# A per-partition scale in the one-hot gate activation, and the first two gate tiles made after the plain phase, in a PEER/attention kernel

## The chip, the cores and the metric

The kernel runs on one core of one Trainium2 chip. The metric is the device time of one execution in microseconds; the time before is 941.41 us, the median of three runs (940.76 to 946.43).

## The reference, cut to what matters

One layer of a diffusion backbone: modulated RMSNorm, an input projection, three mixers, an output projection, and then the PEER feed-forward that this case is about. For 256 tokens `h`:

```python
q = (hb @ w_q).reshape(T, 8, 2, 128)
s = einsum('thpd,hpkd->thpk', q, sub_keys)      # two lists of 128 scores for each head
top_s, top_i = top_k(s, 16)
best_s, best_pos = top_k(cand_s, 16)            # of the 16 x 16 sums
expert = cand_i[best_pos]                       # i0 * 128 + i1, one of 16384
g = softmax(best_s)
act = gelu(einsum('thkd,td->thk', u_tab[expert], hb))
out = einsum('thkd,thk->td', v_tab[expert], g * act)
```

Each token has 128 choices (8 heads x 16). A choice is an index pair (i0, i1) and a gate g.

## The kernel before, in words

**Dense tokens and row tokens.** The first 160 tokens (ND) are computed densely: the activations of all 16384 experts for them, in 128 chunks of 128 experts, are kept in SBUF as A3 (chunk x token), multiplied by a gate that is zero for every expert not chosen, and multiplied by all of peer_v. The last 96 tokens are computed by gathered rows: 96 indirect DMAs bring rows of peer_u (dot products on VectorE, `row_dots`, line 1342), and 96 bring rows of peer_v (weighted sums on VectorE, `row_sums`, lines 1352 and 1355). GpSimd issues these gathers (line 1635), each after VectorE has freed its buffer; from the thirty-third row on there are 8 buffers.

**The u phase, plain part.** TensorE runs `u_chunk` (line 830) for chunks 0 to 87: 8 weight tiles each, into one of 4 banks. SyncE brings each chunk (512 KB) into one of 8 stage buffers as soon as TensorE has read it. ScalarE follows with `gelu_chunk` (line 1108), bank to A3. TensorE may be up to four banks ahead of ScalarE. After chunk 71 TensorE turns `choice` (the indices and gates) with the token on the free axis (line 858), and VectorE copies it into `choice_t` (lines 1532 and 1534). VectorE then does row dots until 39 of them are left.

**The merged part.** For 40 groups g of four tokens, gates are made while the last 40 chunks go on:
- VectorE makes ONE1 for the four tokens with a comparison (`one1`, line 1542).
- ScalarE makes ONE2 for the four tokens: `one2_squares` (line 1123), four ACTIVATEs that give (column - i)^2 with the index as a `[128,1]` bias, and `one2_rest` (line 1130), four that give Relu(gate - 2*square), with the gate as a `[128,1]` bias and -2.0 as a constant scale.
- TensorE's `gates` (line 839) multiplies ONE1 by ONE2 for each token, into bank 4 or 5, and then runs the `u_chunk` of chunk 88 + g.
- ScalarE's `gelu_beside` (line 1115) makes the gelu of the chunk in a side buffer; VectorE's `gate` (line 1550) multiplies A3 by the gates and `multiply` (line 1556) multiplies the chunk's slice by the side buffer; then VectorE does one row dot.

ONE1 and ONE2 have two buffers each. ScalarE's order in the merged part is squares and rest of group g, then the gelu of chunk g - 1, then squares and rest of group g + 1. TensorE's order is gates(g), chunk 88 + g, gates(g + 1). So between the end of chunk g and the start of gates(g + 2), ScalarE has the gelu of that chunk and the eight ACTIVATEs of group g + 2. Groups 0 to 7 are written out, 8 to 39 run in four passes of a hardware loop, where the indices are read through registers.

**The first two groups before the change.** ScalarE makes ONE2 of group 0 after the gelu of chunk 83 and that of group 1 after the gelu of chunk 85, among the last eight gelus, which are written out. Chunks 56 to 79 are a hardware loop of three passes. VectorE makes ONE1 of groups 0 and 1, and then waits for the ones that GpSimd writes into A3 and for all 88 plain gelus (`a_made`), before the first `gate`.

**The v phase.** After the last `gated`, TensorE runs `v_chunk` (line 886) for 128 chunks; the stage buffers are refilled by SyncE and ScalarE. Beside it run the 96 row sums. The end (fold, residual, norm, store) waits for both.

Of the kernel before, what the change touches and what calls it, by code (L numbers as in the profile page):

```python
# [8 lines left out]
ALU = mybir.AluOpType  # L9
# [3 lines left out]
P = 128  # L13
# [3 lines left out]
TB = T // P  # L17
# [14 lines left out]
SLOTS = 8  # L32
BANKS = 4
CHUNKS = NK
GT = 4
# [4 lines left out]
ND = T - SUB * SUBS  # L40
# [4 lines left out]
MERGE = CHUNKS - GROUPS  # L45
A_AT = 8192
SCRATCH = (24576 - A_AT) // ND
EXP_AT = 56
# [207 lines left out]
def build(nc, x_t, ctx_t, cols, rows, sgu_gain, final_gain, constants, sgu_wt, bias_mask, ada_w, w_in,  # L256
# [21 lines left out]
    with ExitStack() as stack:  # L278
        def sbuf(name, shape, dtype=F32):
            return stack.enter_context(nc.sbuf_tensor(name, shape, dtype))  # L280
# [4 lines left out]
        bank = [stack.enter_context(nc.psum_tensor(f"bank{b}", [P, 512], F32)) for b in range(8)]  # L285
# [79 lines left out]
        bias = sbuf("stage", [P, 4, D])  # L365
# [12 lines left out]
        with ExitStack() as views:  # L378
# [31 lines left out]
        choice_t = sbuf("choice_t", [P, 3, ND])  # L410
# [7 lines left out]
        fold4 = con[:, 5 * P + 2:5 * P + 2 + SUB]  # L418
        colv = sbuf("colv", [P, COLS])
        csil = sbuf("csil", [P, KD, 32])  # L420
        mod = sbuf("mod", [P, 5, KD, 2])
        gain1 = sbuf("gain1", [P, KD, 2])
        gain2 = sbuf("gain2", [P, KD])
# [33 lines left out]
        u_read, v_read, a_made = map(sem, ("u_read", "v_read", "a_made"))  # L457
# [4 lines left out]
        ones_made, multiplied, one2_square = map(sem, ("ones_made", "multiplied", "one2_square"))  # L462
        topk_step, shifted, exped, choice_ready, scratch_free, turned, choice_t_ready = map(
            sem, ("topk_step", "shifted", "exped", "choice_ready", "scratch_free", "turned", "choice_t_ready"))
# [87 lines left out]
        def _(pe):  # L552
# [340 lines left out]
                    mm.then_inc(v_read, 1)  # L893

            pe.wait_ge(gated, GROUPS)
            pe.wait_ge(choice_t_ready, 2 * TB)
            for c in range(CHUNKS):
                if c >= MERGE and (c - MERGE) % 8 == 0:
                    pe.wait_ge(multiplied, c - MERGE + 8)
# [45 lines left out]
        def _(act):  # L945
# [160 lines left out]
            def gelu_chunk(j, c):  # L1106
                act.wait_ge(u_read, c + 1)
                act.activation(A3[:, c, :], bank[j % BANKS][:, 0:ND], ACT.Gelu_apprx_tanh).then_inc(a_made, 1)  # L1108

            def gelu_beside(j, n, reused=True):  # L1110

                if reused:
                    act.wait_ge(multiplied, n - 1)
                act.wait_ge(u_read, n + (MERGE + 1))
                act.activation(gelu_buf[:, j % 2, :], bank[j % BANKS][:, 0:ND], ACT.Gelu_apprx_tanh)\  # L1115
                   .then_inc(a_made, 1)

            def one2_squares(j, g, reused=True):

                if reused:  # L1120
                    act.wait_ge(gates_done, g - 1)
                for t in range(GT):
                    last = act.activation(ONE2[:, j % 2, t, :], iota, ACT.Square,  # L1123
                                          bias=choice_t[:, 0, bass.ds(g * GT + t, 1)])
                last.then_inc(one2_square, 1)

            def one2_rest(j, g):
                act.wait_ge(one2_square, g + 1)
                for t in range(GT):
                    last = act.activation(ONE2[:, j % 2, t, :], ONE2[:, j % 2, t, :], ACT.Relu,  # L1130
                                          bias=choice_t[:, 2, bass.ds(g * GT + t, 1)], scale=-2.0)
                last.then_inc(one2_made, 1)

            for j in range(SLOTS):
# [3 lines left out]
                    gelu_chunk(j, i * SLOTS + j)  # L1138
            act.wait_ge(shifted, TB)
            act.activation(choice[:, 2, :, :], choice[:, 2, :, :], ACT.Exp).then_inc(exped, 1)  # L1140
            with act.Fori(EXP_AT // SLOTS, MERGE // SLOTS - 1) as i:
                for j in range(SLOTS):
                    gelu_chunk(j, i * SLOTS + j)
            for j in range(SLOTS):
                gelu_chunk(j, MERGE - SLOTS + j)
                if j == 3:
                    act.wait_ge(choice_t_ready, 2 * TB)
                if j in (3, 5):
                    one2_squares(j // 2 - 1, j // 2 - 1, reused=False)
                    one2_rest(j // 2 - 1, j // 2 - 1)  # L1150
            for j in range(SLOTS):
                if j >= 2:
                    one2_squares(j, j)
                    one2_rest(j, j)
                if j:
                    gelu_beside(j - 1, j - 1, reused=j >= 3)
            def gate_steps(i, j):
                one2_squares(j, i * SLOTS + j)
                one2_rest(j, i * SLOTS + j)
                gelu_beside((j - 1) % SLOTS, i * SLOTS + (j - 1))  # L1160
# [40 lines left out]
        def _(dve):  # L1201
# [134 lines left out]
            def row_dots(n):  # L1336

                s, c = n // ROWS, n % ROWS
                slot = row_slot(n)
                g = gathered[slot]  # L1340
                dve.wait_ge(row_full[slot], 16 * row_fill(n))
                dve.tensor_tensor_reduce(g, g, h2_rows[:, s, :], 1.0, 0.0, ALU.mult, ALU.add, row_dot[:, s, c:c + 1])\  # L1342
                   .then_inc(row_used, 1)

            def row_sums(n):

                s, c = (n - DOTS) // ROWS, (n - DOTS) % ROWS
                slot = row_slot(n)
                g, w = gathered[slot], row_gate[:, s, c:c + 1]
                dve.wait_ge(row_full[slot], 16 * row_fill(n))  # L1350
                if c == 0:
                    dve.tensor_scalar(sums[s][:, :], g, w, None, ALU.mult).then_inc(row_used, 1)
                else:
                    dve.wait_ge(row_used, n)
                    dve.scalar_tensor_tensor(sums[s][:, :], g, w, sums[s][:, :], ALU.mult, ALU.add)\  # L1355
                       .then_inc(row_used, 1)
# [3 lines left out]
            def row(count=1):  # L1360

                for _ in range(count):
                    n = rows_done[0]
                    if n < DOTS:
                        row_dots(n)
                    elif n < 2 * DOTS:
                        row_sums(n)
                    rows_done[0] += 1
# [6 lines left out]
            for kind, n in steps:  # L1375
# [5 lines left out]
                elif kind == "stat1":  # L1381
                    tt = slice(n * T, (n + 1) * T)
# [61 lines left out]
                elif kind == "w_out":  # L1444

                    for b in range(4):
                        name = ("w_out", b)
                        o = full(dve, name)
                        for m in range(2):
                            k = 2 * b + m  # L1450
# [77 lines left out]
            for tb in range(TB):  # L1528
                dve.wait_ge(turned, tb + 1)
                tt = slice(tb * P, min((tb + 1) * P, ND))  # L1530
                n = tt.stop - tt.start
                dve.tensor_scalar(choice_t[:, 0, tt], bank[6 + tb][:, 0:n], -1.0, None, ALU.mult)\
                   .then_inc(choice_t_ready, 1)
                dve.tensor_copy(choice_t[:, 1:3, tt],
                                bank[6 + tb][:, P:3 * P].rearrange("p (n t) -> p n t", n=2)[:, :, 0:n])\
                   .then_inc(choice_t_ready, 1)
            row(DOTS - LATE - rows_done[0])


            def one1(j, g):  # L1540

                dve.tensor_tensor(ONE1[:, j % 2, :, :], iota.unsqueeze(1).broadcast_to([P, GT, NK]),  # L1542
                                  choice_t[:, 1, g * GT:(g + 1) * GT].unsqueeze(2).broadcast_to([P, GT, NK]),
                                  ALU.is_equal).then_inc(one1_made, 1)

            def gate(j, g):

                dve.wait_ge(gates_done, g + 1)
                a = A3[:, :, bass.ds(g * GT, GT)]
                dve.tensor_tensor(a, a, bank[4 + j % 2][:, :].rearrange("p (t c) -> p c t", t=GT), ALU.mult)\  # L1550
                   .then_inc(gated, 1)

            def multiply(j, n):

                dve.wait_ge(a_made, n + (MERGE + 1))
                dve.tensor_tensor(A3[:, n + MERGE, :], A3[:, n + MERGE, :], gelu_buf[:, j % 2, :], ALU.mult)\  # L1556
                   .then_inc(multiplied, 1)

            dve.wait_ge(choice_t_ready, 2 * TB)
            for g in range(GROUPS):  # L1560
                if g >= 2:
                    dve.wait_ge(gates_done, g - 1)
                one1(g, g)
                if g == 1:
                    dve.wait_ge(ones_made, 2)
                    dve.wait_ge(a_made, MERGE)
                if g:
                    dve.wait_ge(multiplied, g - 1)
                    gate(g - 1, g - 1)
                    dve.wait_ge(gated, g)  # L1570
                    multiply(g - 1, g - 1)
                if g:
                    row()
# [163 lines left out]
```

## Time and profile before

| | us |
|---|---|
| median of 3 runs | 941.41 |
| the profiled execution | 940.76 |
| its span | 939.0 |
| TensorE busy | 890.5 (95%) |
| VectorE busy | 535.4 (57%) |
| ScalarE busy | 283.5 (30%) |
| GpSimd busy | 257.4 (27%) |

The profiled execution is 1.76 us longer than its span (what lies around the first and the last instruction) and 0.65 us under the median. The span has three stretches that matter: the plain u phase ends at about 512 us, the merged part runs from 515 to 646 us, and the v phase from 646 to 925 us. "PE" is a matmul and "PEld" a weight load on TensorE.

### The profile page before, as it was taken

To read this page: it belongs to the slowest core of one execution; us is meant where nothing else is said; L and a number is where in the kernel's file an instruction comes from. 1 tells how busy PE (TensorE), PEld (TensorE's weight loads), DVE (VectorE), ACT (ScalarE), POOL (GpSimd) and SP (SyncE) were. 2 spreads that over 40 slices of the span, in tenths; PEclk is the share of its full clock that TensorE was granted. 3 is DMA by queue.
4 is the path that set the end of the run, shared out by engine and by line. 5 is a ranking of instruction groups with operands and counts; after the bars stand their busy time and mean duration, and the time that the engine had idled before them with its cause. 6 is when DMAs were issued, how large, how long until landed. Compare 5 with 4: busy or idle time off the path is not lost.

```text
span 939.0 us, 18081 instructions
## 1 busy us (share of the span) xinstructions
PE 890.5 (95%) x6850; PEld 837.9 (89%) x6850; DVE 535.4 (57%) x1035; ACT 283.5 (30%) x687; POOL 257.4 (27%) x239
## 2 busy tenths in 40 slices
PE   5799999869999999999998999999999999999995
PEld 3587998449798999999997999999999999999995
DVE  1446104657458976997445688888434343334347
ACT  3453223664633211112113688883000000000002
POOL 0000000330133033346543233364432323222320
PEclk9597999999999999999999899999999999999998
DMA  9674583204336489999999999999999999999993
GB/s 371 289 269 171 189 314 136 89 7 175 135 135 270 119 244 384 410 409 409 409 409 410 409 362 326 320 320 353 408 409 408 409 409 409 409 409 409 409 409 131
DMA packets 73984, 292.74 MB, mean 312 GB/s; under 512 B 9026, under 2 KB 9154, under 8 KB 67396
## 3 DMA queue, kind: packets, MB, share of 16 engines
q1 hardware_dynamic: 36868, 159.67, 44.1%
q0 software_dynamic: 28416, 100.78, 28.4%
q10 hardware_dynamic: 8640, 31.46, 8.4%
q8 instruction: 42, 0.69, 0.3%
q14 instruction: 18, 0.15, 0.0%
HBM read 290.72 MB, written 1.05 MB: 311 GB/s over the span
## 4 chain that ended last, share of the span: by engine, by line
PE 36%; DMA 32%; DVE 5%; ACT 3%; issue 2%; POOL 1%; ACTq 0%; DVEq 0%; SPq 0%
DMA A<-in_peer_v,row_expert 25%; PE bank L830 24%; PE bank L839 4%; DMA A<-in_peer_u,row_expert 4%; DVE sum L1355 3%; DMA stage<-in_peer_u_t 2%; PE bank L573 1%; PE bank L575 1%; PE bank L574 1%; PE bank L724 1%; PE bank L727 1%; PE bank L726 1%; POOL A L1635 1%; PE bank L779 1%; PE bank L757 1%
## 5 line engine op out<-in xcount | busy, mean ns | idle before, releaser
L830 PE MATMUL bank<-A,stage 128*128 128x160 f32 x2048 | 291.3, 301 | 2.3 <-DMA stage<-in_peer_u_t 1.1
L830 PEld LDWEIGHTS bank<-A,stage 128*128 128x128 f32 x2048 | 282.0, 191 | 5.9 <-issue 5.6
L886 PE MATMUL bank<-A,stage 128*128 128x160 f32 x2048 | 278.4, 299 | 0.0
L886 PEld LDWEIGHTS bank<-A,stage 128*128 128x128 f32 x2048 | 278.2, 190 | 0.0
L1355 DVE SCALAR_TENSOR_TENSOR sum<-A,row_gate,sum 128x1024 f32<-128x1024 f32 x81 | 104.0, 1284 | 132.8 <-DMA A<-in_peer_v,row_expert 131.1
L1635 POOL DMA_INDIRECT A<-in_peer_u,row_expert x80 | 91.1, 1138 | 140.7 <-DVE row_dot L1342 133.4
L1635 POOL DMA_INDIRECT A<-in_peer_v,row_expert x84 | 82.6, 984 | 166.2 <-DVE sum L1355 148.8
L1342 DVE CUSTOM_DVE_ANT_0 A<-A 128x1024 f32<-128x1024 f32 x80 | 97.4, 1220 | 46.9 <-DMA A<-in_peer_u,row_expert 46.8
L1175 ACT ACTIVATE A<-bank 128x480 f32<-128x480 f32 x1 | 0.6, 570 | 276.3 <-PE bank L886 276.3
L1108 ACT ACTIVATE A<-bank 128x160 f32 (+1 forms) x88 | 26.7, 303 | 155.2 <-PE bank L830 155.2
L575 PE MATMUL bank<-h_hi,ring_low 128*128 128x256 f32 x256 | 73.1, 286 | 0.0
L1196 POOL TENSOR_TENSOR ring_low<-A,hi 128x512 fp32r<-128x512 f32 x4 | 5.2, 1323 | 175.7 <-ACT hi L1014 175.7
L1130 ACT ACTIVATE gate_buf<-gate_buf,choice_t 128x128 f32<-128x128 f32 x160 | 51.2, 390 | 4.4
L1123 ACT ACTIVATE gate_buf<-con,choice_t 128x128 f32<-128x128 f32 x160 | 50.7, 391 | 0.6 <-issue 0.6
L575 PEld LDWEIGHTS bank<-h_hi,ring_low 128*128 128x128 f32 x256 | 49.9, 195 | 0.0
L839 PE MATMUL bank<-gate_buf 128*128 128x128 f32 x320 | 44.6, 283 | 4.6 <-DVE gate_buf L1542 3.6
L839 PEld LDWEIGHTS bank<-gate_buf 128*128 128x128 f32 x320 | 39.7, 194 | 8.6 <-issue 8.5
L1275 DVE TENSOR_TENSOR ring_low<-A,hi 128x2048 fp32r<-128x2048 f32 x6 | 13.8, 2292 | 40.0 <-ACT hi L1002 40.0
L593 PE MATMUL bank<-A,csil 128*32 128x256 f32 x384 | 28.9, 426 | 3.7 <-DMA A<-in_ada_w 3.7
L1626 POOL TENSOR_TENSOR ring_low<-A,yn_low 128x2048 fp32r<-128x2048 f32 x3 | 13.8, 4600 | 61.3 <-ACT yn_low L1002 61.3
L1550 DVE TENSOR_TENSOR A<-A,bank 128x512 f32<-128x512 f32 x40 | 27.1, 679 | 1.8 <-PE bank L839 1.8
L1556 DVE TENSOR_TENSOR A<-A,choice 128x160 f32<-128x160 f32 x40 | 13.0, 325 | 25.2 <-ACT choice L1115 25.2
(234 smaller groups left out, 1240.6 us busy)
## 6 DMA issues: line engine op xcount, KB each, us to landing
stage<-in_peer_u_t SPq DMA_DIRECT2D x128, 512.0 KB, 11.1
stage<-in_peer_v SPq DMA_DIRECT2D x68, 512.0 KB, 7.7
stage<-in_peer_v ACTq DMA_DIRECT2D x60, 512.0 KB, 8.3
A<-in_ada_w SPq DMA_DIRECT2D x24, 1024.0 KB, 7.0
A<-in_w_in SPq DMA_DIRECT2D x11, 1024.0 KB, 4.8
A<-in_w_q SPq DMA_DIRECT2D x8, 1024.0 KB, 5.5
A<-in_w_out SPq DMA_DIRECT2D x4, 1024.0 KB, 6.9
stage<-in_bias_mask SPq DMA_DIRECT2D x1, 2048.0 KB, 12.7
```

Of the source, the lines that this page charges most:

```text
L575: mm = pe.matmul(o, a_lo, b_hi, start=False, stop=(k == KD - 1))
L593: mm = pe.matmul(o[q, 0:BLK], csil[:, k, :], w[:, k, :], start=(k < 4), stop=(k >= 4), tile_position=(0, 32 * (k % 4)))
L830: mm = pe.matmul(o, stage[j][:, k * P:(k + 1) * P], H2[:, k, 0:ND], start=(k == 0), stop=(k == KD - 1))
L839: mm = pe.matmul(bank[4 + j][:, t * NK:(t + 1) * NK], ONE1[:, j, t, :], ONE2[:, j, t, :], start=True, stop=True)
L886: mm = pe.matmul(bank[b][:, n * ND:(n + 1) * ND], stage[c % SLOTS][:, m * P:(m + 1) * P], A3[:, c, :], start=(c == 0 and n == 0), stop=(c ...
L1108: act.activation(A3[:, c, :], bank[j % BANKS][:, 0:ND], ACT.Gelu_apprx_tanh).then_inc(a_made, 1)
L1123: last = act.activation(ONE2[:, j % 2, t, :], iota, ACT.Square, bias=choice_t[:, 0, bass.ds(g * GT + t, 1)])
L1130: last = act.activation(ONE2[:, j % 2, t, :], ONE2[:, j % 2, t, :], ACT.Relu, bias=choice_t[:, 2, bass.ds(g * GT + t, 1)], scale=-2.0)
L1342: dve.tensor_tensor_reduce(g, g, h2_rows[:, s, :], 1.0, 0.0, ALU.mult, ALU.add, row_dot[:, s, c:c + 1])\
L1355: dve.scalar_tensor_tensor(sums[s][:, :], g, w, sums[s][:, :], ALU.mult, ALU.add)\
L1550: dve.tensor_tensor(a, a, bank[4 + j % 2][:, :].rearrange("p (t c) -> p c t", t=GT), ALU.mult)\
L1635: pool.indirect_dma_start(gathered[slot], None, peer_u if n < DOTS else peer_v, bass.IndirectOffsetOnAxis(ap=row_expert[:, s, c:c + 1], ax ...
```

## The change

The scale of `one2_rest` becomes a `[128,1]` operand, minus the gate, so that it gives Relu(gate - gate*square). These values are new: `less_gate`, in the memory of a tile (`csil`) that is used only at the kernel's start, made by VectorE with one more TENSOR_SCALAR for each of the two blocks of tokens. The three engines that wait for `choice_t_ready` now wait for a count of 6 instead of 4. ONE2 of groups 0 and 1 is made after the gelu of chunk 87. The eight written-out gelus become a fourth pass of the loop. VectorE's two waits stand before ONE1 of group 0.

```diff
+        less_gate = csil[:, :, :].rearrange("p k v -> p (k v)")[:, 0:ND]
...
-            pe.wait_ge(choice_t_ready, 2 * TB)
+            pe.wait_ge(choice_t_ready, 3 * TB)
...
                     last = act.activation(ONE2[:, j % 2, t, :], ONE2[:, j % 2, t, :], ACT.Relu,
-                                          bias=choice_t[:, 2, bass.ds(g * GT + t, 1)], scale=-2.0)
+                                          bias=choice_t[:, 2, bass.ds(g * GT + t, 1)],
+                                          scale=less_gate[:, bass.ds(g * GT + t, 1)])
...
-            with act.Fori(EXP_AT // SLOTS, MERGE // SLOTS - 1) as i:
+            with act.Fori(EXP_AT // SLOTS, MERGE // SLOTS) as i:
                 for j in range(SLOTS):
                     gelu_chunk(j, i * SLOTS + j)
+            act.wait_ge(choice_t_ready, 3 * TB)
             for j in range(SLOTS):
-                gelu_chunk(j, MERGE - SLOTS + j)
-                if j == 3:
-                    act.wait_ge(choice_t_ready, 2 * TB)
-                if j in (3, 5):
-                    one2_squares(j // 2 - 1, j // 2 - 1, reused=False)
-                    one2_rest(j // 2 - 1, j // 2 - 1)
-            for j in range(SLOTS):
-                if j >= 2:
-                    one2_squares(j, j)
-                    one2_rest(j, j)
+                one2_squares(j, j, reused=j >= 2)
+                one2_rest(j, j)
                 if j:
                     gelu_beside(j - 1, j - 1, reused=j >= 3)
...
+                dve.tensor_scalar(less_gate[:, tt], bank[6 + tb][:, 2 * P:2 * P + n], -1.0, None, ALU.mult)\
+                   .then_inc(choice_t_ready, 1)
...
-            dve.wait_ge(choice_t_ready, 2 * TB)
+            dve.wait_ge(choice_t_ready, 3 * TB)
+            dve.wait_ge(ones_made, 2)
+            dve.wait_ge(a_made, MERGE)
             for g in range(GROUPS):
                 if g >= 2:
                     dve.wait_ge(gates_done, g - 1)
                 one1(g, g)
-                if g == 1:
-                    dve.wait_ge(ones_made, 2)
-                    dve.wait_ge(a_made, MERGE)
```

## Rows read from the trace of the kernel before

**Rows 1.** The page: the chain by line, and the v phase's matmuls.

```profile
DMA A<-in_peer_v,row_expert 25%; PE bank L830 24%; PE bank L839 4%; DMA A<-in_peer_u,row_expert 4%; DVE sum L1355 3%; DMA stage<-in_peer_u_t 2%; PE bank L573 1%; PE bank L575 1%; PE bank L574 1%; PE bank L724 1%; PE bank L727 1%; PE bank L726 1%; POOL A L1635 1%; PE bank L779 1%; PE bank L757 1%
...
L886 PE MATMUL bank<-A,stage 128*128 128x160 f32 x2048 | 278.4, 299 | 0.0
```

**Rows 2.** The chain in order of time, 470 to 530 us: start, us, piece.

```profile
472.50 0.29 DVE choice_t L1532
...
473.12 0.10 DVE choice_t L1532
...
494.33 18.95 DMA A<-in_peer_u,row_expert
...
514.53 0.61 DVE gate_buf L1542
...
515.39 2.05 PE bank L839 x8
```

**Rows 3.** Timeline of ScalarE, 498 to 524 us: start, us, instruction, [idle before, releaser].

```profile
501.79 1.26 ACT L1123 ACTIVATE gate_buf<-con,choice_t 128x128 f32<-128x128 f32 x4
503.09 1.28 ACT L1130 ACTIVATE gate_buf<-gate_buf,choice_t 128x128 f32<-128x128 f32 x4
...
511.85 0.30 ACT L1108 ACTIVATE A<-bank 128x160 f32<-128x160 f32 x1 [2.18 <-PE bank L830]
521.56 0.30 ACT L1115 ACTIVATE choice<-bank 128x160 f32<-128x160 f32 x1 [9.40 <-PE bank L830]
```

**Rows 4.** Timeline of ScalarE in the merged part, 546 to 551 us.

```profile
546.99 0.30 ACT L1115 ACTIVATE choice<-bank 128x160 f32<-128x160 f32 x1 [0.57 <-PE bank L830]
547.19 1.27 ACT L1123 ACTIVATE gate_buf<-con,choice_t 128x128 f32<-128x128 f32 x4
548.59 1.28 ACT L1130 ACTIVATE gate_buf<-gate_buf,choice_t 128x128 f32<-128x128 f32 x4
550.06 0.30 ACT L1115 ACTIVATE choice<-bank 128x160 f32<-128x160 f32 x1 [0.19 <-PE bank L830]
```

**Rows 5.** Timeline of TensorE in the merged part, from 549 us.

```profile
549.99 0.97 PEld L839 LDWEIGHTS bank<-gate_buf 128*128 128x128 f32 x8 [0.21 <-issue]
...
550.98 2.34 PE L830 MATMUL bank<-A,stage 128*128 128x160 f32 x16
```

**Rows 6.** Groups of ScalarE by form: shapes, count, busy us, mean ns, idle before.

```profile
L1130 ACT ACTIVATE gate_buf<-gate_buf,choice_t 128x128 f32<-128x128 f32 x160 | 51.2, 390 | 4.4
...
L1078 ACT ACTIVATE A<-A,mod 128x256 f32<-128x256 f32 x8 | 3.9, 497 | 2.5 <-DVE A L1464 2.5
...
L990 ACT ACTIVATE h_hi<-A 128x256 fp32r<-128x256 f32 x8 | 3.1, 404 | 0.0
```

**Rows 7.** Timeline of ScalarE, 243 to 244 us: two forms back to back.

```profile
243.01 0.49 ACT L1078 ACTIVATE A<-A,mod 128x256 f32<-128x256 f32 x1
243.41 0.40 ACT L990 ACTIVATE h_hi<-A 128x256 fp32r<-128x256 f32 x1
243.72 0.49 ACT L1078 ACTIVATE A<-A,mod 128x256 f32<-128x256 f32 x1
```

**Rows 8.** Line 1130: register instructions of ScalarE's queue, min/median/max ns.

```profile
L1130 ACTq FUSED_REGOPS  x128: 46/46/46, 542.1 to 641.9; - x128
```

**Rows 9.** Timeline of ScalarE, 475 us: a table load in the gelu loop.

```profile
475.09 1.28 ACT L1108 ACT_TABLE_LOAD   x1 [2.51 <-PE bank L830]
```

**Rows 10.** Stretches: length, busy (count) of PE, PEld, DVE, ACT, POOL, clock, DMA.

```profile
484.00:511.00 27.00, 25.56 (x172) 23.41 (x172) 12.22 (x21) 7.78 (x27) 9.37 (x10) 1.00 1.03 409
511.80:515.30 3.50, 0.01 (x1) 0.00 (x0) 2.17 (x6) 0.30 (x1) 1.43 (x2) 0.87 1.03 410
515.30:521.30 6.00, 5.91 (x24) 5.94 (x25) 1.13 (x2) 0.00 (x0) 0.65 (x1) 0.51 1.02 408
543.00:647.00 104.00, 102.95 (x778) 99.67 (x777) 85.50 (x162) 86.43 (x284) 43.34 (x45) 1.00 0.96 333
647.00:924.00 277.00, 277.00 (x2041) 277.00 (x2040) 121.40 (x98) 0.57 (x1) 85.17 (x88) 1.00 1.01 401
```

## The prediction

> **What bounds the kernel now.** I read the page's chain first. Two things end it: the gathers of peer_v rows with the sums on VectorE, and TensorE in the chunks of the u phase [rows 1]. Next the stretches, to see which resource is full where [rows 10]. In the v phase (647 to 924 us) TensorE is busy for all 277.00 us at a granted clock of 1.00, and its matmuls had no idle time at all before them [rows 1]; the DMA engines move 401 GB/s there against 409 where they are fullest. So the v phase is a block of fixed length, 278.4 us, that begins when the last gates are in: a late start is paid in full. The row sums beside it run on the same DMA bandwidth and move with it, because only eight of their rows can be fetched ahead. What the change touches lies before this block, at the entrance to the merged part and inside it.
>
> The entrance: the chain in order of time goes through the gathers of peer_u rows (two links of some 19 us) to VectorE's first ONE1, and then to TensorE's first gates [rows 2]. TensorE stands still from 511.8 to 515.3 us, because VectorE comes late from its row dots; after that gap its clock is granted at 0.51, the lower level of 1.2 GHz, and the first gates and chunk take 6.1 us, from 515.39 until the chunk's gelu can start at 521.56 [rows 2, 3, 10]. ScalarE is not what is late here: it has ended its last plain gelu at 512.15 and then idles 9.40 us [rows 3].
>
> Inside the merged part TensorE looks full (102.95 of 104.00 us), which would hide anything that ScalarE does. The timelines say otherwise. ScalarE's group ends at 548.59 + 1.28 = 549.87, and TensorE's weight load for the next gates begins at 549.99, 0.12 us later, with 0.21 us of idle time before it [rows 4, 5]. That chunk's matmuls end at 550.98 + 2.34 = 553.32. The gelu before it started at 546.99, so this link is 6.33 us from a gelu's start to the end of the chunk two groups on, and with the gap of about 0.04 us to the next gelu 6.37 us. Two groups in 6.37 us is 3.18 us each. TensorE's own share of a group, with the weights loaded ahead, would be shorter. The loop that sets the pace is therefore: chunk's end, gelu, four squares, four Relus, gates, chunk. ScalarE's 2.88 us (from 546.99 to 549.87) are all in it, and they are counted once in two groups.
>
> **The change part by part.**
>
> (1) *The scale as a per-partition operand.* The trace of before has no ACTIVATE with two such operands. It has pairs that differ by one: on 128x256, line 1078 with a `[128,1]` bias has a mean of 497 ns, line 990 with none 404 ns, so one operand costs 93 ns [rows 6]. This is not hidden when they follow one another: from the start of the one with the operand to the next is 243.41 - 243.01 = 0.40 us, from the other 243.72 - 243.41 = 0.31 us [rows 7]. Line 1130 already has one (390 ns, four in 1.28 us, about 0.30 us apart) [rows 4, 6]. Bounds for the second: nothing, if both are fetched together; and 93 + 46 ns, if the register instruction for its address (46 ns, one for each ACTIVATE of line 1130 now) [rows 8] no longer fits beside the work. Not below nothing, since the form with more operands is the slower one in the only pair. I take the nearest row, 93 ns, so 4 x 0.093 = 0.372 us for each group.
>
> The ScalarE page of the Trainium skill ("ScalarE: Activation LUTs", section "What ACT_TABLE_LOAD costs") says that each `[128,1]` pointer operand adds about 93 ns and that back-to-back ACTIVATEs overlap by about 93 ns. The trace agrees for the first operand; no row of before shows a second one. By the page the sum would be the same 0.372 us, and a reading in which the second comes free would be wrong.
>
> How much of it is paid: groups 2 to 39 go round the loop named above, that is 38 groups, or 19 links one after the other (even and odd groups run side by side). 19 x 0.372 = 7.07 us. In the idle-time view ScalarE would seem to have room (0.57 and 0.19 us before two gelus, [rows 4]), but that idle time is its wait for the chunk in the same loop; it is no cover. ScalarE alone, about 2.8 us a group and 3.2 with the operand, stays under the new pace of 3.18 + 0.19 = 3.37 us.
>
> (2) *A second register instruction* for the new operand's address, in the loop's 32 groups. Those of the second to fourth ACTIVATE have 0.30 us of work to hide behind; that of the first stands in the open, since 548.59 - 547.19 = 1.40 us although the squares take 1.27 us. One more of 46 ns for each of 16 links: 0.74 us. From nothing (if both addresses are computed in one) to 0.046 x 4 x 16 = 2.94 us.
>
> (3) *VectorE's two added TENSOR_SCALARs* from PSUM. Their likes, line 1532 on 128x128 and on 128x32, hold the chain for 0.29 and 0.10 us [rows 2]. They stand before row dots whose gathers lead to the first ONE1, so 0.39 us is the upper bound; nothing is the lower, as the gathers run on full DMA (409 GB/s, [rows 10]) and a buffer freed later may only trim the queue. The chain goes through the neighbours, so I take 0.3 us. No other engine is behind them; the waits for the count of 6 are met some 28 us before anyone comes to them.
>
> (4) *ONE2 of groups 0 and 1 later.* Before, they lay between gelus where TensorE was up to four banks ahead and DMA-bound, so their removal gives nothing. Now: last gelu at 511.85, squares 0.20 us later (as 547.19 stands to 546.99, [rows 4]), Relus 1.30 after that (503.09 - 501.79, [rows 3]), and they end 1.28 + 0.37 later, at 515.00. With the 0.12 us to the weight load that is 515.12; VectorE's ONE1 lets TensorE start at 515.39 [rows 2, 3]. A tie with 0.27 us left: nothing. If this cover goes (the loop's exit on ScalarE is now in this stretch), each tenth later is paid in full; I keep 1 us as the upper bound, some half of the 2.18 us that ScalarE idles before such a gelu, in which the exit of the loop lay hidden before. Group 1 then ends near 518, when TensorE is still on its slow chunk until 521.5, and the 9.40 us of idle time covers both groups (5.9 us).
>
> (5) *VectorE's waits moved up.* Behind them stand only ONE1 of groups 0 and 1. The gelu they wait for ends at 512.15, VectorE gets there at 514.53 [rows 2, 3]: nothing, with 2.4 us of cover. *A fourth pass of the gelu loop*: each pass holds a table load of 1.28 us ahead of its first gelu [rows 9], so one more, behind which TensorE has three banks free of 2.2 to 2.6 us each: nothing.
>
> Sum: 7.07 + 0.74 + 0.3 = 8.1 us; 940.76 + 8.1 = 948.9 us. That is against the profiled execution, which lies 0.65 us under the median of the runs shown; both are within the spread of such runs, and I give 949.0.
>
> **The rivals.**
>
> *The second operand comes free* (not slower). One mechanism: the scale is fetched beside the bias, so that line 1130 stays at 390 ns. Then 0.3 us is left, 941.1 us. It decides already if line 1130's mean stays below about 400 ns. For it: nothing in the trace shows that two fetches are serial. Against it: the first one is visible in full in both duration and spacing.
>
> *Register work and entrance at their upper bounds.* All second register instructions in the open (2.94 in place of 0.74) and 1 us at the entrance: 7.07 + 2.94 + 0.4 + 1.0 = 11.4, 952.2 us. For it: from squares to Relus the loop takes 1.40 us, the written-out groups 1.30 [rows 3, 4]. Against it: the spacing inside four ACTIVATEs is about 0.30 us with or without a register instruction.
>
> *The clock falls in the merged part.* TensorE's wait grows by some 0.2 us a group. If that brought its clock to 1.2 GHz as the gap before 515 us did, each such episode would cost what that one did: 6.1 us for a gates and a chunk against 3.2, so 3 us. Four of them, one for each pass of the loop, give 949 + 12 = 961 us. Against it: from 484 to 511 us TensorE worked 25.56 of 27.00 us, with gaps before every chunk, at a clock of 1.00 [rows 10].
>
> **How the numbers follow.** Forecast 0.72; operand free 0.13; upper bounds 0.10; clock 0.05. The predicted time is the forecast's. Its own spread is about 1.5 us either way. The range leaves out the free operand and the clock: 943.0 (half of the operand's cost hidden) to 952.2. A change of 1% (9.4 us) is about what a measurement of this kernel can tell from none. Slower by over 1% means above 950.8: the clock's 0.05, most of the upper bounds' (0.08), and a tenth of the forecast's (0.07), 0.20 together. Faster by over 1% has no mechanism: 0.02. The rest is 0.78.
>
> **What would show it.** Line 1130's mean goes from 390 to about 483 ns, four of them from 1.28 to 1.65 us, while line 1123 stays at 391. Two groups of the merged part take 6.7 instead of 6.37 us, and the v phase starts near 654 instead of 646 us and lasts 278 us again. ScalarE's idle time before line 1115 shrinks by less than the operands add. At the entrance the first gates start between 515.4 and 515.8 us and are still released by VectorE; were it ScalarE's line 1130, step 4 was wrong. The prediction is wrong if line 1130 is longer but the spacing of gates is not (then TensorE was the bound), or if the spacing does not move because the operand is free.

## The result, and the profile after

In the first comparison the changed kernel takes 950.62 us (median of 8, 948.6 to 952.5), the kernel before 942.49 us: a ratio of 1.0084, with a 95% interval of 1.0064 to 1.0103, 8.1 us more. In a later comparison on another chip it took 950.79 against 938.43 us, 1.0120 (1.0098 to 1.0142), 12.4 us more. The changed kernel takes the same time in both; it is the kernel before that differs (942.49 and 938.43 us).

The profiled execution after took 952.36 us, with a span of 950.5 us. First the page: ScalarE's two gate groups and the v phase's matmuls (answers to [rows 1, 6]).

```profile
L1131 ACT ACTIVATE gate_buf<-gate_buf,choice_t,csil 128x128 f32<-128x128 f32 x160 | 65.9, 482 | 5.3 <-ACT gate_buf L1124 5.0
...
L1124 ACT ACTIVATE gate_buf<-con,choice_t 128x128 f32<-128x128 f32 x160 | 50.7, 390 | 0.6 <-issue 0.6
...
L887 PE MATMUL bank<-A,stage 128*128 128x160 f32 x2048 | 278.4, 299 | 0.0
```

Line 1131 is what was line 1130. Its mean has gone from 390 to 482 ns: the second operand costs 92 ns. Line 1124 (the squares, one operand as before) stays, and the v phase takes the same 278.4 us. Next the timelines of ScalarE and of TensorE after, in the merged part (answers to [rows 4, 5]):

```profile
552.18 0.30 ACT L1116 ACTIVATE choice<-bank 128x160 f32<-128x160 f32 x1 [0.33 <-PE bank L831]
552.38 1.27 ACT L1124 ACTIVATE gate_buf<-con,choice_t 128x128 f32<-128x128 f32 x4
553.80 1.65 ACT L1131 ACTIVATE gate_buf<-gate_buf,choice_t,csil 128x128 f32<-128x128 f32 x4 [0.16 <-ACT gate_buf L1124]
555.36 0.28 ACT L1116 ACTIVATE choice<-bank 128x160 f32<-128x160 f32 x1
```

```profile
548.84 1.13 PE L840 MATMUL bank<-gate_buf 128*128 128x128 f32 x8 [0.54 <-issue]
...
552.00 1.13 PE L840 MATMUL bank<-gate_buf 128*128 128x128 f32 x8
...
555.60 1.13 PE L840 MATMUL bank<-gate_buf 128*128 128x128 f32 x8 [0.30 <-issue]
```

The four Relus take 1.65 us where they took 1.28. Gates start at 548.84 and 555.60, so two groups take 6.76 us where they took about 6.37. ScalarE ends its group at 553.80 + 1.65 = 555.45, and the gates start 0.15 us later, with idle time before them. From a gelu's start to that point is 3.27 us instead of 2.88.

At the entrance the chain in order of time runs now through ScalarE (answers to [rows 2]):

```profile
517.16 1.27 ACT gate_buf L1124 x4
518.43 0.03 issue
518.46 1.66 ACT gate_buf L1131 x4
520.11 0.14 issue
520.25 1.83 PE bank L840 x8
522.07 3.15 PE bank L831 x16
525.22 0.02 issue
525.24 0.30 ACT choice L1116
```

And the stretches after (answers to [rows 10]; the columns are the same):

```profile
520.20:526.00 5.80, 5.75 (x33) 5.79 (x34) 1.04 (x3) 3.48 (x11) 0.00 (x0) 0.71 1.03 410
...
547.00:657.50 110.50, 104.51 (x778) 100.00 (x777) 86.28 (x163) 97.13 (x284) 43.09 (x45) 1.00 0.91 308
657.50:936.00 278.50, 278.45 (x2050) 278.21 (x2049) 121.98 (x98) 1.06 (x4) 86.52 (x89) 1.00 1.01 400
```

The merged part is where the time went. The gelu of chunk 88 starts at 525.24 and the v phase at 657.6, 132.4 us; before they were 521.56 and 646.2, 124.6 us. That is 7.8 us more, and TensorE's clock stays at 1.00 in it. The rest of the 11.5 us between the two spans lies ahead of that gelu: the u phase starts at 315.8 us instead of 313.3, although the two kernels have the same instructions up to there, and the first gates come 204.4 us after that start instead of 202.1. From the first gates to the gelu it is the other way round, 5.0 us instead of 6.2, because more of this stretch of the kernel before ran at the lower clock (granted 0.51 there, 0.71 after).

### The profile page after: what moved, and what is told of

It reads as the page before. It is cut to its first block, busy times and chain, and to the rows that moved or that the text cites. A ratio compares the mean times of both kernels' runs of the same rounds, so it can differ in the third digit from the quotient of the medians.

```text
span 950.5 us, 18102 instructions
## 1 busy us (share of the span) xinstructions
PE 894.1 (94%) x6850; PEld 839.8 (88%) x6850; DVE 535.7 (56%) x1037; ACT 298.3 (31%) x688; POOL 259.9 (27%) x239
## 4 chain that ended last, share of the span: by engine, by line
PE 40%; DMA 28%; ACT 4%; DVE 4%; issue 3%; POOL 1%; ACTq 0%; DVEq 0%; SPq 0%
PE bank L831 27%; DMA last_row<-in_peer_v,row_expert 25%; PE bank L840 4%; DVE sum L1350 2%; DMA stage<-in_peer_u_t 2%; PE bank L574 1%; PE bank L575 1%; PE bank L576 1%; DMA A<-in_peer_v,row_expert 1%; PE bank L728 1%; PE bank L727 1%; PE bank L725 1%; ACT gate_buf L1131 1%; ACT gate_buf L1124 1%; PE bank L780 1%
## 5 line engine op out<-in xcount | busy, mean ns | idle before, releaser
L887 PE MATMUL bank<-A,stage 128*128 128x160 f32 x2048 | 278.4, 299 | 0.0
L1350 DVE SCALAR_TENSOR_TENSOR sum<-A,row_gate,sum 128x1024 f32<-128x1024 f32 x81 | 104.0, 1284 | 133.2 <-DMA A<-in_peer_v,row_expert 128.0
L1131 ACT ACTIVATE gate_buf<-gate_buf,choice_t,csil 128x128 f32<-128x128 f32 x160 | 65.9, 482 | 5.3 <-ACT gate_buf L1124 5.0
```

What stands on the lines that cost most here:

```text
L887: mm = pe.matmul(bank[b][:, n * ND:(n + 1) * ND], stage[c % SLOTS][:, m * P:(m + 1) * P], A3[:, c, :], start=(c == 0 and n == 0), stop=(c ...
```

## The experiments

Three theories were tested first. Theory 1: the second operand's 92 ns stand in a loop of waits (chunk's end, gelu, squares, Relus, gates, chunk), in which a group's ScalarE work is paid once in two groups. Theory 2: the rise comes from the moved ONE2 and waits. Theory 3: the pace is set by an engine's busy time. Two more, 4 and 5, are stated in the expectation of the run that tests them. The times of each run are given beside the kernel before, run in the same comparison. Each is the median of 5 to 13 executions, or of 17 to 29 for the kernel before.

**The scale alone.** The order of the kernel before, with

```diff
-                                          bias=choice_t[:, 2, bass.ds(g * GT + t, 1)], scale=-2.0)
+                                          bias=choice_t[:, 2, bass.ds(g * GT + t, 1)],
+                                          scale=less_gate[:, bass.ds(g * GT + t, 1)])
```

> Only the per-partition scale, with the tile it needs and the waits for it; the order of ScalarE's and VectorE's work is that of the kernel before. Theory 1 (the second operand costs 93 ns an ACTIVATE, and the loop chunk - gelu - squares - Relus - gates pays it once in two groups): line 1131 at about 483 ns, two groups in 6.76 us instead of 6.37, 7 to 8 us slower than before, all of it inside the merged part. Theory 2 (the rise comes from the moved ONE2 and the waits at the entrance and before it): within 2 us of before, although line 1131 is longer.

946.08 against 938.57 us, 1.0080 (1.0057 to 1.0104): 7.5 us. Theory 1 holds and theory 2 cannot be the whole. Its merged part took 137.3 us in the profile, from the first gates to the v phase, as after (137.4); by the same measure the kernel before took 130.8. All three began at the lower clock. Three later profiles began with no gap of TensorE, and show the operand's price alone: 128.0 us in the kernel before, 135.1 and 135.6 us with the second operand (`before_again`, `static_scale`, `scale_again`), so 7.1 and 7.6 us.

**The moved work alone.** The change with the constant scale put back:

```diff
-                                          scale=less_gate[:, bass.ds(g * GT + t, 1)])
+                                          scale=-2.0)
```

> Only the moved work: the fourth pass of the gelu loop, ONE2 of groups 0 and 1 after the plain gelus, VectorE's waits ahead; the scale is the constant -2.0 again. Theory 1: within 1.5 us of before, line 1130 at 390 ns and two groups in 6.37 us; the first gates may wait some tenths for ScalarE. Theory 2: 5 to 8 us slower than before.

943.16 against 938.57 us, 1.0054 (1.0038 to 1.0070): 4.6 us. Neither theory expected that much beside the other's share. The merged part is 128.0 us, as in the kernel before when it begins with no gap. What differs is the start of it; the chain of this kernel there:

```profile
517.45 1.27 ACT gate_buf L1124 x4
518.72 0.02 issue
518.75 1.28 ACT gate_buf L1131 x4
520.03 0.14 issue
520.17 1.13 PE bank L840 x8
```

and TensorE's timeline at the same place:

```profile
520.17 1.13 PE L840 MATMUL bank<-gate_buf 128*128 128x128 f32 x8 [3.06 <-ACT gate_buf L1131]
```

TensorE stands 3.06 us for ScalarE's first ONE2.

**A fixed column as the scale.** As the scale alone, but the operand is a column that holds -2.0:

```diff
+                dve.memset(less_gate[:, tt], -2.0).then_inc(choice_t_ready, 1)
...
-                                          bias=choice_t[:, 2, bass.ds(g * GT + t, 1)], scale=-2.0)
+                                          bias=choice_t[:, 2, bass.ds(g * GT + t, 1)],
+                                          scale=less_gate[:, 0:1])
```

> As the kernel with the scale alone, but the operand is one fixed column that holds -2.0, so that its address needs no register. Theory 1 with the operand's fetch as the whole price: the same 482 ns and the same 7 to 8 us as with the gate's own column. If the register for the address is part of it, the distance from the squares to the Relus goes back to 1.40 us and up to 1 us of the rise goes away. Theory 2: within 2 us of before.

945.76 us, 1.0076 (1.0050 to 1.0102), 7.2 us; line 1131 is again at its longer duration, four in 1.65 us. So the price is that of having the operand, whatever it holds and whether or not its address comes from a register. The registers' share is too small to see in the time. The rows of line 1131 are, in this kernel and then after,

```profile
L1131 ACTq FUSED_REGOPS  x128: 46/46/46, 541.9 to 647.3; - x128
```

```profile
L1131 ACTq FUSED_REGOPS  x128: 55/58/60, 546.9 to 652.9; - x128
```

The change has as many register instructions as before, each some 12 ns longer, not one more for each ACTIVATE. From the squares to the Relus is 1.40 us here (548.70 - 547.30) and 1.42 after (553.80 - 552.38).

**The squares ahead of the wait.** The kernel before, with one exchange in ScalarE's order; the written-out groups and the tail likewise:

```diff
                 one2_squares(j, i * SLOTS + j)
+                gelu_beside((j - 2) % SLOTS, i * SLOTS + (j - 2))
                 one2_rest(j, i * SLOTS + j)
-                gelu_beside((j - 1) % SLOTS, i * SLOTS + (j - 1))
```

> The kernel before with ScalarE's order in the merged part changed to squares(g), gelu(g-2), Relus(g): the squares stand ahead of the wait for the chunk. Theory 1 (a loop of waits sets the pace, not the busy time of an engine): the path from chunk's end to the next gates is 1.4 us shorter, TensorE is then the bound at about 3.07 us a group, and the kernel is 4 to 6 us faster than before with the same instructions. Theory 3 (ScalarE's or TensorE's busy time sets the pace): no change within 1 us.

933.52 against 938.57 us, 0.9954 (0.9934 to 0.9974): 5.0 us faster. Theory 3 in its form "busy time sets the pace" falls. ScalarE's and TensorE's timelines of this kernel:

```profile
547.59 0.30 ACT L1115 ACTIVATE choice<-bank 128x160 f32<-128x160 f32 x1 [0.43 <-PE bank L830]
547.78 1.27 ACT L1130 ACTIVATE gate_buf<-gate_buf,choice_t 128x128 f32<-128x128 f32 x4
548.95 1.27 ACT L1123 ACTIVATE gate_buf<-con,choice_t 128x128 f32<-128x128 f32 x4
550.65 0.30 ACT L1115 ACTIVATE choice<-bank 128x160 f32<-128x160 f32 x1 [0.43 <-PE bank L830]
```

```profile
547.38 1.05 PE L839 MATMUL bank<-gate_buf 128*128 128x128 f32 x8
...
550.45 1.05 PE L839 MATMUL bank<-gate_buf 128*128 128x128 f32 x8
```

The squares of the next group now run while TensorE is still on its chunk. ScalarE idles 0.43 us before each gelu, and it is true spare time here: a group takes 3.07 us, with no idle time before TensorE's gates. The merged part falls to 123.4 us.

**The kernel before once more.**

> The kernel before itself, to see what differs from one execution to the next with no edit: the start of the u phase (313.4 to 316.8 us in the six profiles so far), the end of the plain chunks (511.8 to 517.1) and TensorE's gap before the first gates (3.6, 1.9, 1.4 and 0 us in the four profiles with ONE2 made early, 3.1 and 3.4 in the two with it made late). Every theory: no difference from before beyond its interval, and a gap set by VectorE or none, not by ScalarE.

939.20 against 938.80 us, 1.0004 (0.9988 to 1.0021). Its profile has no gap. VectorE and TensorE at the entrance:

```profile
515.29 1.29 DVE L1542 TENSOR_TENSOR gate_buf<-con,choice_t 128x512 f32<-128x512 f32 x2
...
517.01 1.05 PE L839 MATMUL bank<-gate_buf 128*128 128x128 f32 x8
```

VectorE's first ONE1 began there at 515.29, before the last chunk's end, and ONE2 of group 0 was ready. In the profile of before on which the prediction rests TensorE waited 3.6 us at this place, and worked at the lower clock after it. So that profile shows one of several ways in which the entrance can go. From the start of the u phase to the start of the v phase it took 332.9 us, this one 329.2: its entrance had cost it 3.7 us.

**The moved work without the fourth pass of the loop.**

```diff
-            with act.Fori(EXP_AT // SLOTS, MERGE // SLOTS) as i:
+            with act.Fori(EXP_AT // SLOTS, MERGE // SLOTS - 1) as i:
                 for j in range(SLOTS):
                     gelu_chunk(j, i * SLOTS + j)
+            for j in range(SLOTS):
+                gelu_chunk(j, MERGE - SLOTS + j)
```

> The kernel with the moved work and the constant scale, but its last eight plain gelus written out again, so without the fourth pass of the loop and its table load. Theory 4 (the price of the move is the entrance: ScalarE's 3.1 us from the last chunk's end stand before the first gates in every execution, where VectorE's lateness stood in some): gap of 3.1 us released by ScalarE, 3 to 5 us slower than before, as with the loop. Theory 5 (the price is the loop's fourth pass): within 1.5 us of before.

942.44 against 938.80 us, 1.0041 (1.0022 to 1.0060): 3.6 us, with a gap of 2.95 us that ScalarE releases. Theory 4 holds, theory 5 falls: the gap is there without the loop's fourth pass. This kernel and the one with that pass (3.6 and 4.6 us) differ by 1.0 us, which their intervals do not tell from none.

**The changed kernel with the squares ahead.** The exchange above, in the changed kernel.

> The changed kernel with ScalarE's order squares(g), gelu(g-2), Relus(g). Theory 1: the wait loop loses 1.4 us and no longer binds; ScalarE's own work is then nearest, 3.15 to 3.25 us a group in the hardware loop, a little more than TensorE's 3.07, so the merged part falls from 137 to some 130 us and the kernel is within 3 us of before, 5 to 7 us faster than the changed one. Theory 3 (busy time is the bound): as the changed kernel, 8 us slower than before.

940.74 against 938.80 us, 1.0022 (1.0008 to 1.0035), some 10 us faster than the changed kernel in its second comparison. In its profile the merged part took 123.7 us against 137.4, so all of what the operand had added is gone and more. ScalarE's work of a group fitted into 3.07 us there (3.15 to 3.25 was expected), and TensorE set the pace. But this profile is of its fastest execution (935.42 us), 5.3 us under the median; where the others lost that time is not shown.

**A second operand for the squares too.**

```diff
                     last = act.activation(ONE2[:, j % 2, t, :], iota, ACT.Square,
-                                          bias=choice_t[:, 0, bass.ds(g * GT + t, 1)])
+                                          bias=choice_t[:, 0, bass.ds(g * GT + t, 1)], scale=ones[:, 0:1])
```

> The changed kernel with the squares' scale a fixed column of ones too (it was the constant 1), so that a second operand is added to all eight ACTIVATEs of a group. Theory 1: line 1124 goes from 390 to 482 ns and two groups from 6.76 to 7.13 us if only the wait loop counts; ScalarE's own work is then 3.5 to 3.6 us a group and may take over as the bound, two groups in 7.1 to 7.3 us; 15 to 19 us slower than before. If the operand's cost were paid only where TensorE is idle anyway, less than 3 us would be added to the changed kernel.

959.16 against 938.80 us, 1.0215 (1.0191 to 1.0239): 20.4 us, a little over the range given from theory 1. The group of line 1124, and TensorE's timeline:

```profile
L1124 ACT ACTIVATE gate_buf<-con,choice_t 128x128 f32<-128x128 f32 x160 | 65.5, 482 | 0.6 <-issue 0.6
```

```profile
556.00 1.13 PE L840 MATMUL bank<-gate_buf 128*128 128x128 f32 x8 [0.23 <-ACT gate_buf L1131]
...
563.13 1.13 PE L840 MATMUL bank<-gate_buf 128*128 128x128 f32 x8 [0.23 <-ACT gate_buf L1131]
```

390 has become 482 ns here too, and two groups take 7.13 us, 0.37 more than after: the wait loop's arithmetic, 4 x 0.092 once in two groups. From 550 to 570 us the chain of this kernel runs through ScalarE alone, so its own work is at the bound as well.

**Both halves side by side.** The changed kernel and the scale alone once more.

> The changed kernel once more, on the chip and in the rounds of the next three, because the two halves of the change measured 7.5 us (scale) and 4.6 us (moved work) by themselves, but 8.1 us together on another chip. If the halves add up (one is paid in the merged part, the other at the entrance): 11 to 12 us slower than before. If 8.1 us holds: about 8 us, and something of one half is hidden by the other.

> The scale alone once more, beside the changed kernel. Halves that add up: 7 to 8 us slower than before and 3 to 5 us faster than the changed kernel. Otherwise within 1.5 us of the changed kernel.

The changed kernel: 950.79 against 938.43 us, 12.4 us slower. The scale alone: 945.93 us, 1.0080 (1.0058 to 1.0103), 7.5 us slower, the same as the first time. Beside the 4.6 us of the moved work that makes 12.1 us: in this order of ScalarE's work the halves add up. The changed kernel's TensorE at the entrance, and that of the scale alone:

```profile
518.54 2.05 PE L840 MATMUL bank<-gate_buf 128*128 128x128 f32 x8 [3.43 <-ACT gate_buf L1131]
520.37 4.12 PE L831 MATMUL bank<-A,stage 128*128 128x160 f32 x16
```

```profile
515.33 1.05 PE L840 MATMUL bank<-gate_buf 128*128 128x128 f32 x8
516.22 2.34 PE L831 MATMUL bank<-A,stage 128*128 128x160 f32 x16
```

A gap of 3.43 us, and then gates and chunk at the lower clock (granted 0.50 from 519 to 523 us); against no gap and the full clock.

**Each half with the squares ahead.**

> The scale alone with ScalarE's order squares(g), gelu(g-2), Relus(g). Theory 1: with the wait loop out of the way and TensorE's 3.07 us a group still just over ScalarE's 3.06, the second operand costs nothing: within 1.5 us of the 933.5 us that the kernel before gave with this order, 4 to 6 us faster than before. Theory 3 (the operand's busy time is paid wherever it stands): 2 to 3 us slower than before.

934.51 against 938.43 us, 0.9946 (0.9925 to 0.9967). The operand that cost 7.5 us costs 1.0 us over the 933.52 us of the same order without it, from another comparison, and the intervals of the two ratios (0.9946 and 0.9954) overlap almost wholly. In the two profiles the way from the u phase's start to the v phase's start is 323.7 us with the operand and 323.4 without. The stretch from 540 to 620 us of this kernel:

```profile
540.00:620.00 80.00, 80.00 (x629) 80.00 (x628) 69.67 (x133) 78.84 (x237) 33.51 (x35) 1.00 1.01 375
```

ScalarE is busy 78.84 of 80 us, which is more than in the changed kernel, and TensorE all of them. The operand is as long as ever; it is no longer in a loop of waits. It has used up the cover, though: without the operand ScalarE was busy 68.79 us in the same stretch of this order.

> The moved work with the constant scale, and the order squares(g), gelu(g-2), Relus(g). If the move is paid at the entrance alone (theory 4): a gap of 3.0 us before the first gates released by ScalarE, 123 to 124 us for the merged part, and 3 to 5 us slower than the kernel before with this order (so 0 to 2 us faster than before). If the move's price were part of the wait loop in the merged part, it would be gone: 4 to 6 us faster than before.

937.34 against 938.43 us, 0.9984 (0.9969 to 1.0000): 3.8 us slower than the same order with ONE2 made early. TensorE at its entrance:

```profile
516.56 2.05 PE L840 MATMUL bank<-gate_buf 128*128 128x128 f32 x8 [3.10 <-ACT gate_buf L1131]
```

Its merged part took 125.7 us (123 to 124 was expected, 123.4 is that of the same order with ONE2 made early); 1.7 us of the difference are its first gates and chunk, 4.77 us at the lower clock instead of 3.07. The gap and the lower clock after it are there although the wait loop is gone, so the move's price is at the entrance, not in the pace of the merged part.

All profiles together: in the seven with ONE2 made early TensorE's gap before the first gates was 3.58, 1.91, 1.42 us and four times none, on average 1.0; in the seven with ONE2 made late it was 2.95 to 3.80 us, on average 3.3, always released by ScalarE. The first gates then took more than 1.13 us, the sign of the lowered clock, in two of the first seven and in four of the others. The stretch from the u phase's start to the v phase's start gathers all that the change touches. It took 332.9 and 329.2 us in the two profiles of the kernel before, and 341.8 and 341.7 us in the two of the changed kernel.

## Why the prediction was right, and where it was not

The forecast was 949.0 us, 8.1 us over the profiled execution of 940.76; measured were 950.62 us and, over the median of 942.49, 8.1 us. The time is right, and so is the larger part of the mechanism. That the rise agrees to a tenth is luck: one step, worth 3.6 to 4.6 us, was put at nothing, the three counted ones came to 7.5 us together where 8.1 had been counted, and the kernel before was some 4 us slower in this comparison than in all later ones. In the later comparison the rise is 12.4 us.

*What bounds the kernel*: right. The wait loop between ScalarE and TensorE sets the pace although TensorE looks full, shown by the order with the squares ahead, which gains 5.0 us with the same instructions. The v phase moved by its start alone (278.4 us before and after).

*Step 1, the operand*: right. 92 ns against 93, four Relus in 1.65 us, two groups in 6.76 us where 6.37 + 0.37 = 6.74 was the forecast of this step. 7.07 us were forecast, the scale alone measured 7.5 us twice, and the merged part by itself grew by 7.1 and 7.6 us. The Trainium skill ("ScalarE: Activation LUTs", section "What ACT_TABLE_LOAD costs") gives some 93 ns for each such operand. The runs agree, now for a second operand too (390 to 482 ns), in the Relu and in the Square. The idle time of ScalarE was no cover, as said: it became one only when the order was changed.

*Step 2, the register instruction*: mis-sized. There is no second one; the one that was there grew from 46 to 58 ns, and the way from squares to Relus from 1.40 to 1.42 us. 0.74 us were counted; over 16 links 0.02 us are 0.3.

*Step 3, VectorE's added instructions*: not tested by itself. The scale alone has them too, and its 7.5 us leave, beside the 7.07 and 0.3, no more than some tenths; 0.3 us were counted.

*Step 4, ONE2 of groups 0 and 1 later*: this step failed. The forecast called it a tie and put it at nothing; the runs show 3.6 to 4.6 us. The time for ScalarE's ONE2 was worked out well, as 3.15 us from the start of the last plain gelu. In the profile after, that gelu is

```profile
516.96 0.30 ACT L1109 ACTIVATE A<-bank 128x160 f32 x1 [1.87 <-PE bank L831]
```

and ONE2 ends at 520.11, again 3.15 us later. But this was held against one execution, in which VectorE's first ONE1 came so late that TensorE waited 3.58 us anyway. In the six other profiles with ONE2 made early TensorE waited 1.91 us, 1.42 us or not at all, and then at least some 1.5 us, and mostly all, of ScalarE's 3.0 to 3.4 us is new, with the lower clock on top in some. The sign that the prediction named for this failure came true: the first gates were released by ScalarE's line 1131, at 520.25 us, where 515.4 to 515.8 and VectorE had been forecast.

The same step bears on the two comparisons. From the u phase's start to the v phase's start the changed kernel took 8.9 us more than the profile of before with the gap, and 12.5 us more than the one without, close to the 8.1 and 12.4 us of the medians. So a first comparison in which the kernel before mostly had the gap and the low clock would give its result. That this was so is not shown: only one of its executions has a profile.

*Step 5*: a cost of the loop's pass can't be told from none. VectorE's moved wait did bind, as its cover of 2.4 us came from the same late execution. In the profile after:

```profile
517.39 1.29 DVE L1539 TENSOR_TENSOR gate_buf<-con,choice_t 128x512 f32<-128x512 f32 x2 [2.20 <-ACT A L1109]
```

It cost nothing by itself, since ScalarE's ONE2 ended later still, at 520.11.

*The rivals.* The free operand is ruled out by the 482 ns. The clock did not fall inside the merged part, 1.00 over 110.5 us with TensorE 94.6% busy; it fell at the entrance, where the rival did not look. The upper bounds were wrong about the registers (2.94 us where 0.3 was found) and, at 1 us, too low about the entrance. The range's lower end, 943.0, does not follow from its reason: with half of the operand's cost hidden the forecast's own sum gives 949.0 - 3.5 = 945.5 us.

*Open*: with the squares ahead, scale and move together came to 940.74 us, 7.2 us over 933.52, while the two by themselves cost 1.0 and 3.8. The profiles account for 3.6 us of it: from the u phase's start to the v phase's start they give 327.0 us for both together and 323.4 us for neither, and 3.3 us of this lie at the entrance. The other 3.6 us are in executions that have no profile. Where the u phase starts (312.8 to 317.7 us over the fourteen profiles) varies from one execution to the next, in the kernel before as well (313.3 and 315.8); what sets it was not looked for.

## What to carry to other kernels

Where two engines hand work back and forth, follow one item round the loop and add up what it passes; busy shares and idle times do not show that loop, and whatever stands in it is paid, here once in two groups because the ONE2 of a group is made two groups after the chunk it waits for. Before a change in instructions, look for a piece of the item's work that does not need what the engine waits for, and put it ahead of the wait: the squares ahead of the gelu gained 5.0 us and hid the costly operand almost wholly (0.3 us left in the profiles, 1.0 us in the medians). The kernel before with that order (933.52 us, 0.9954) beats both kernels. And a cover that is read from one execution at a point where a race decides (who is late, VectorE or TensorE) must be priced as if it were zero too: look at more than one profile there, or keep the uncovered price in the sum.

## What the runs showed of the hardware

A per-partition scale beside a per-partition bias costs an ACTIVATE 92 ns (390 to 482) even when it holds one constant for all and its address is fixed, and it costs that in the distance to the next one too (four in 1.65 us instead of 1.28). A gap of TensorE of some 3 us was followed by the lower of its two clock levels in some executions and not in others: the same gates took 2.05 us at a granted clock of 0.50 after a gap of 3.10 us, and 1.13 us at 1.00 after one of 3.06 us. A gap of 1.91 us was followed by the lower level too (1.62 us for the gates in `scale_only`, granted 0.51 from 515 to 517 us). So the same wait has two prices.
